# Two directions of a linear recurrence on the two halves of the array, row buffers at the end of three gathers, and two stages' loads

## The chip, the cores and the metric

The kernel runs on one core of a Trainium2 chip. The time is device microseconds (us), the median of repeated runs. TensorE is PE in the profile (its weight loads PEld), VectorE DVE, ScalarE ACT, GpSimd POOL, SyncE SP. SP, ACT and POOL issue the DMAs. All data are float32.

## The reference, cut to what matters

Two transformer blocks work on 256 tokens of width 1024. The first has two layers (with a context of 256 tokens in the first), each with a token mix and a product-key expert layer: every token picks 128 of 16384 experts, the kernel gathers their rows of two tables (4 KB each, "down" and "up"), takes the dot product of the token with each down row, puts it through gelu and a gate, and adds up the weighted up rows. The second block has attention, a bidirectional linear recurrence, and an expert layer of the same kind with its own tables.

```
def step(state, inp):                      # forward, and once more in reverse
    r_t, w_t, k_t, v_t, kk_t, a_t = inp
    sa = einsum('bhvk,bhk->bhv', state, -kk_t)
    state = (state * w_t[:, :, None, :]
             + sa[..., :, None] * (kk_t * a_t)[..., None, :]
             + v_t[..., :, None] * k_t[..., None, :])
    y = einsum('bhvk,bhk->bhv', state, r_t)
    return state, y
...
a = einsum('tkd,td->tk', peer_down[ee], hh)     # ee: 128 expert numbers a token
act = gg * gelu(a)
out = einsum('tk,tkd->td', act, peer_up[ee])
```

## The kernel before

Each engine has a class (`Vector`, `Tensor`, `Scalar`, `Pool`, `Sync`) that walks through the same `main` (L444) and emits only its own instructions. A stage is a generator; `weave` runs a front stage and puts `rate` units of a back stage between two of its steps, the same way on every engine, so the order of the work is fixed by the code and by that rate. PSUM has eight banks of 512 columns; a stage takes banks in turn from a ring (`step` has banks 0 to 2, `prep` 3 to 5), and waits until a bank's last reader has drained it. Weight blocks of 2 MB go into slots; slots 0 and 1 have memory of their own, slot 2 lies on the four buffers `K.ds`.

**Gathers.** `gather` handles one expert of all 128 tokens of a tile at a time: POOL fetches a down row and an up row, 0.5 MB each, into one of four buffers each (`K.ds`, `K.us`); DVE takes the dot product of the down row (L741); every 16 experts ACT applies gelu and DVE the gates; ACT makes a diagonal matrix of an expert's weights; PE multiplies it with the up row into PSUM (in odd tiles only the first half of the columns, the other half is DVE's). The up rows run 18 experts (`LAG`) behind the down rows, so at the end of each gather come 18 up rows alone. There are three gathers: four tiles, two tiles, and two tiles in the second block. `fold` ends a tile. Behind the first gather comes `x_second`, whose `modulate` starts with three vectors that ACT fetches (`take_vectors`).

**The recurrence** works on chunks of 32 tokens, with four heads of 32 tokens as 128 rows. The forward direction's 64 channels lie on partitions 0 to 63 and the reverse direction's on 64 to 127. A batch (`bt`, four of them) is two chunks of each direction. `prep` (L1995) makes what a batch needs that doesn't depend on the state: five gram products (`gram`), which DVE masks (`masked`), an inverse by powers of the masked matrix (`prod`), with evictions by ACT (`power`) and sums into `Q` by DVE. `steps` (L2074) runs through the chunks: a product with the state (`TA`, 64 rows) and `tl` times the values (128 rows), an eviction `UE` by DVE, the outputs into `b3`, and the state's update into `b2` (64 columns of the array), which DVE adds to the state and scales by the decay. `place` adds a chunk's outputs to two banks kept for that. `steps` of a batch is woven with `prep` of the next. The weave in front of it runs `recur` and the first `prep` with attention as its back.

**Behind it** come `close` (a group norm on DVE, and transposes), `project` with the weights `w_out_2` in two blocks, `modulate`, and the queries of the last gather.

## Time and profile before

| | |
|---|---|
| median of 3 runs | 4604.28 us (4602.84 to 4610.88) |
| the profiled execution | 4609.44 us |
| its span in the trace | 4607.6 us |
| PE busy | 3479.5 us (76%) |
| DVE busy | 2590.0 us (56%) |
| POOL busy | 1998.9 us (43%) |
| ACT busy | 831.7 us (18%) |
| mean DMA rate | 288 GB/s |

The trace counts a float32 matmul as two records and two weight loads. A row of the timeline gives the start, the length, the engine, the line of the kernel, the operation with its operands, how many it merges (x), and in brackets the idle time before it and what ended that. The first gather ends near 2150 us, the second near 3172, the recurrence runs from about 3453 to 3763, and the last gather ends near 4603.

### The profile page before, as it was taken

The page shows a single profiled execution, that of the slowest core. Times are in us where ns is not written, and L with a number is a line of the kernel's source. Part 1 is how long each engine was busy: PE and PEld are TensorE (multiplying, and loading weights), DVE is VectorE, ACT ScalarE, POOL GpSimd, SP SyncE. Part 2 cuts the span into 40 slices and gives each one's busy share as a digit, 9 for nine tenths or more (in the row PEclk, how much of TensorE's full clock was granted, in tenths as well). Part 3 has the DMA queues.
Part 4 walks back from the last instruction along what each step waited for, and adds up shares of the span by engine and source line. Part 5 has one row for each costly group of instructions (what it writes and reads, how often), then busy time and mean ns, then how long its engine had stood idle before and what let it go on. Part 6 is the DMA issues. An engine that isn't in the chain of part 4 may idle for free.

```text
span 4607.6 us, 34532 instructions
## 1 busy us (share of the span) xinstructions
PE 3479.5 (76%) x10470; PEld 1735.8 (38%) x10470; DVE 2590.0 (56%) x5497; ACT 831.7 (18%) x1973; POOL 1998.9 (43%) x2112
## 2 busy tenths in 40 slices
PE   6895868987786778876858766777679865877777
PEld 3483424553342235522434222212366643422111
DVE  1414695565877336674356755674443335667776
ACT  1311113111211122211211111111221101111111
POOL 0101666554666435574126764572000001676775
PEclk9997999988789889966979997757678987999656
DMA  5434999999999989998769998996000014999998
GB/s 188 170 148 167 360 342 358 360 377 341 382 338 374 373 327 344 407 400 315 245 222 353 401 386 314 403 407 234 12 1 1 1 52 164 348 402 361 405 408 341
DMA packets 385359, 1328.12 MB, mean 288 GB/s; under 512 B 38956, under 2 KB 44332, under 8 KB 381592
## 3 DMA queue, kind: packets, MB, share of 16 engines
q0 software_dynamic: 306432, 1115.88, 63.7%
q1 hardware_dynamic: 72592, 187.29, 11.0%
q10 hardware_dynamic: 6152, 22.74, 1.4%
q8 instruction: 87, 1.43, 0.1%
q14 instruction: 96, 0.79, 0.0%
HBM read 1324.59 MB, written 1.17 MB: 288 GB/s over the span
## 4 chain that ended last, share of the span: by engine, by line
PE 22%; DMA 14%; DVE 6%; POOL 5%; issue 4%; ACT 2%; DVEq 0%; ACTq 0%; POOLq 0%; SPq 0%
PE ps L1456 21%; DMA arena<-in_peer_up,arena 6%; POOL arena L2704 5%; DMA arena<-in_peer_v,arena 4%; DVE arena L728 3%; DVE arena L741 2%; ACT arena L2148 2%; DMA arena<-in_peer_u,arena 1%; DMA arena<-in_peer_down,arena 1%; PE ps L1462 1%; DMA arena<-in_ada_w 1%; DMA arena<-mod_scratch 0%; ACT L2148 0%; DVE arena L749 0%; DMA arena<-in_w_out 0%
## 5 line engine op out<-in xcount | busy, mean ns | idle before, releaser
L1456 PE MATMUL ps<-arena 128*128 128x512 f32 (+11 forms) x9732 | 3368.5, 522 | 902.9 <-DMA arena<-in_peer_up,arena 348.7
L1456 PEld LDWEIGHTS ps<-arena 128*128 128x128 f32 (+5 forms) x9732 | 1639.2, 197 | 2567.2 <-issue 1407.0
L741 DVE SCALAR_TENSOR_TENSOR arena<-arena,ps 128x1024 f32<-128x1024 f32 x1024 | 1240.9, 1216 | 512.1 <-DMA arena<-in_peer_down,arena 343.0
L2704 POOL DMA_INDIRECT arena<-in_peer_down,arena x768 | 740.7, 964 | 809.5 <-DVE arena L741 324.6
L2704 POOL DMA_INDIRECT arena<-in_peer_up,arena x768 | 731.5, 952 | 551.3 <-PE ps L1456 385.1
L2148 ACT ACTIVATE arena<-arena 128x128 f32<-128x128 f32 (+5 forms) x1250 | 448.2, 384 | 2009.7 <-PE ps L1456 953.8
L2704 POOL DMA_INDIRECT arena<-in_peer_u,arena x256 | 243.3, 950 | 817.5 <-DVE arena L745 724.2
L741 DVE SCALAR_TENSOR_TENSOR ps<-arena,ps 128x512 f32<-128x512 f32 x508 | 382.9, 754 | 147.5 <-DMA arena<-in_peer_up,arena 109.0
L2148 ACT ACTIVATE arena<-ps 128x512 f32<-128x512 f32 (+3 forms) x381 | 196.3, 515 | 1251.9 <-PE ps L1456 891.0
L728 DVE TENSOR_TENSOR arena<-ps,arena 128x512 f32<-128x512 f32 (+3 forms) x192 | 131.2, 683 | 472.7 <-PE ps L1456 430.7
L1462 PE MATMUL ps<-arena 128*128 128x128 f32 (+2 forms) x738 | 137.4, 326 | 219.2 <-DVE arena L728 152.2
L2704 POOL DMA_INDIRECT arena<-in_peer_v,arena x256 | 241.5, 944 | 128.0 <-PE ps L1456 87.7
L728 DVE TENSOR_TENSOR arena<-arena 128x512 f32<-128x512 f32 (+9 forms) x412 | 253.4, 615 | 45.1 <-ACT arena L2148 26.6
L728 DVE TENSOR_TENSOR arena<-arena,ps 128x256 f32<-128x256 f32 (+2 forms) x142 | 78.4, 552 | 309.8 <-PE ps L1456 286.6
L1462 PEld LDWEIGHTS ps<-arena 128*128 128x128 f32 (+2 forms) x738 | 101.4, 162 | 297.7 <-issue 187.5
L2148 ACT ACTIVATE arena<-ps,arena 128x256 f32<-128x256 f32 (+2 forms) x140 | 71.0, 507 | 416.7 <-PE ps L1456 380.7
L745 DVE COPY arena<-ps 128x512 f32<-128x512 f32 (+5 forms) x69 | 39.6, 574 | 173.3 <-PE ps L1456 142.5
L2148 ACT ACT_TABLE_LOAD x88 | 112.9, 1283 | 83.7 <-DVE arena L736 42.3
L2667 POOL DMA_DIRECT2D arena<-in_w_mod x16 | 12.5, 784 | 182.7 <-PE ps L1456 120.8
L1063 DVE MAX8 arena<-ps 128x8 f32<-128x128 f32 x128 | 28.7, 286 | 111.1 <-PE ps L1456 109.5
L741 DVE DVE_READ_ACCUMULATOR arena<-arena,ps 128x1 f32 x1024 | 83.9, 82 | 0.0
L741 DVE SCALAR_TENSOR_TENSOR arena<-arena 128x1024 f32<-128x1024 f32 (+6 forms) x67 | 46.8, 699 | 50.5 <-DMA arena<-mod_scratch 47.2
(35 smaller groups left out, 539.6 us busy)
## 6 DMA issues: line engine op xcount, KB each, us to landing
arena<-in_w_mod SPq DMA_DIRECT2D x16, 2048.0 KB, 18.2
arena<-in_gate_blocks SPq DMA_DIRECT2D x16, 2048.0 KB, 10.3
arena<-in_w_in SPq DMA_DIRECT2D x14, 2048.0 KB, 15.8
arena<-in_w_pq SPq DMA_DIRECT2D x12, 2048.0 KB, 10.1
arena<-in_ada_w POOLq DMA_DIRECT2D x24, 1024.0 KB, 5.7
arena<-in_w_mod POOLq DMA_DIRECT2D x16, 1024.0 KB, 6.0
arena<-in_w_out SPq DMA_DIRECT2D x8, 2048.0 KB, 13.2
arena<-in_gate_blocks SPq DMA_DIRECT2D x8, 1792.0 KB, 9.9
```

The lines of the kernel that those rows point to most:

```text
L728: self.e.tensor_tensor(o, a, b, op).then_inc(*(inc or self.inc(self.S.vec)))
L741: self.e.scalar_tensor_tensor(o, a, s, b, op0, op1, accum_out=accum).then_inc(*(inc or self.inc(self.S.vec)))
L745: self.e.tensor_copy(o, a).then_inc(*(inc or self.inc(self.S.vec)))
L1063: e.max(v[j][:, 0:8], src[j]).then_inc(*self.inc(S.vec))
L1456: return self.e.matmul(o, l, r, start=start, stop=stop)
L1462: ins = self.e.transpose(o, x, self.K.ident)
L2148: self.e.activation(o, i, f, bias=bias, scale=scale, accum_out=accum).then_inc(*(inc or self.inc(self.S.act)))
L2667: self.e.dma_start(K.wbuf[2][:, 2048 * half:2048 * half + 2048].rearrange("p (k n) -> p k n", n=512), rows[:, 4 * half:4 * half + 4, :]).t ...
L2704: self.e.indirect_dma_start(out=o, out_offset=None, in_=table, in_offset=bass.IndirectOffsetOnAxis(ap=idx.bitcast(U32), axis=0)).then_inc( ...
```

## The change

**The recurrence.** `grams` is a stage of its own in front of `prep`: five units, each with one gram product of both directions, the matmuls of the two directions in turn (one reads partitions 0 to 63, the other 64 to 127) and into two banks. The masked results of the reverse direction have memory of their own (`K.GRAM`). `prep` keeps eight units a direction. `steps` takes both directions of a chunk together: four units a batch instead of eight, the matmuls of the two directions in turn, one bank `b2` for both state updates, and one addition and one scaling on 128 partitions for both, with the decay copied into one tile first. The weave's rate goes from 2.25 to 5.25. `recur` orders its sums over time so that the directions take turns.

PE, one whole batch in the weave, as it was; here and below `free` is a bank drained, `128x256` a product of a step, `128x128` one of `prep` or a gram, `64x256` a state update and L1462 a transpose:

```order
L1456 MATMUL ps<-arena 128x128 x16
L1456 MATMUL ps<-arena 128x256 x4
L1456 MATMUL ps<-arena 128x128 x24
L1456 MATMUL ps<-arena 128x256 x6
L1456 MATMUL ps<-arena 64x256 x4
L1456 MATMUL ps<-arena 128x128 x4
```

and the batch's first half now, with what each waits for:

```order
L1492 MATMUL ps<-arena 128x256 [waits free1,state,free0,free4]
L1492 MATMUL ps<-arena 128x256 x7
L1492 MATMUL ps<-arena 128x512
L1492 MATMUL ps<-arena 128x512 [waits free2]
L1492 MATMUL ps<-arena 128x128 [waits free3]
L1492 MATMUL ps<-arena 128x128 x7
L1492 MATMUL ps<-arena 128x128 [waits free5]
L1492 MATMUL ps<-arena 128x128 x7
L1492 MATMUL ps<-arena 128x128 [waits free4,free3]
L1492 MATMUL ps<-arena 128x128 x7
L1492 MATMUL ps<-arena 128x256 [waits free1,free0]
L1492 MATMUL ps<-arena 64x256 x8
```

The products of a step stand in groups of eight and twelve, and the grams as five groups of eight in a row, each group behind the draining of banks 3 to 5.

PE, the last batch, where nothing is woven in, as it was:

```order
L1456 MATMUL ps<-arena 128x256 [waits state]
L1456 MATMUL ps<-arena 128x256 x3
L1456 MATMUL ps<-arena 128x512 [waits free0]
L1456 MATMUL ps<-arena 128x256 [waits state,free2]
L1456 MATMUL ps<-arena 128x256 [waits free1]
L1456 MATMUL ps<-arena 128x256 x5
L1456 MATMUL ps<-arena 64x256 x4
```

and now:

```order
L1492 MATMUL ps<-arena 128x256 [waits state,free1,free0]
L1492 MATMUL ps<-arena 128x256 x7
L1492 MATMUL ps<-arena 128x512
L1492 MATMUL ps<-arena 128x512 [waits free2]
L1492 MATMUL ps<-arena 128x256 [waits free1,free0]
L1492 MATMUL ps<-arena 128x256 x11
L1492 MATMUL ps<-arena 64x256 x8
```

A chunk waits once for the state instead of once per direction, and the twelve output products wait for both `UE` evictions (banks 0 and 1) at their start.

**The gathers.** The last 18 up rows go in turn into `K.us` and into the down buffers, which have no more down rows to take (`up_place`); POOL's waits follow that (`freed`), and a load into slot 2 waits until the up rows are used. Of the 19 fetches in a row with which a gather ends on POOL, four in the middle now wait for a dot product (`down`) and the others, as before, for an up row's use.

**Two stages' loads.** In the last tile of the first gather ACT also issues the three vectors of `x_second`'s `modulate`. SP issues the two blocks of `w_out_2` at the fence in front of `close`, not behind it, into slots 0 and 1.

```diff
+    def down_place(self, s):
+
+        x = self.base + LAG // 2 * self.gathers + s
+        return self.K.ds[x % ND], (self.S.down_in[x % ND], 16 * (x // ND + 1))
+
+    def up_place(self, u, total):
+
+        i = u - (total - LAG)
+        if i < 0 or i % 2 == 0:
+            x = self.base - LAG // 2 * self.gathers + (u if i < 0 else total - LAG + i // 2)
+            return self.K.us[x % NU], (self.S.up_in[x % NU], 16 * (x // NU + 1))
+        return self.down_place(total + i // 2)
 
     def folded(self, n):
...
-            self.weave(self.steps(bt % 2, bt), preps(bt + 1) if bt < 3 else iter(()), 2.25, rings=("step", "prep"))
+            self.weave(self.steps(bt % 2, bt), preps(bt + 1) if bt < 3 else iter(()), 5.25, rings=("step", "prep"))
         self.fence()
-        self.ring = self.rings["most"]
+        self.ring, self.slot = self.rings["most"], self.slots["two"]
         self.run(self.close())
         self.fence()
...
+        def masked(masks):
+            b = self.bank()
             self.wait_ge(*self.full(b))
...
+        for d in range(2):
+            masked(((d, K.GRAM[d]["L"]), (4 + d, K.GRAM[d]["LO"])))
+        yield
+        for d in range(2):
+            masked(((1 - d, K.GRAM[d]["Mt"]),))
+        yield
+        for d in range(2):
+            masked(((6 + d, K.GRAM[d]["LK"]),))
+        yield
+        for name in ("rb", "rk"):
+            for d in range(2):
+                masked(((3 - d, K.PD[bf][d][name]),))
+            yield
+
+    def prep(self, bf, d, chunks):
...
-                yield
+            decay = K.small[:, 8 * ci:8 * ci + 8]
             for d in range(2):
                 pr, c = slice(64 * d, 64 * d + 64), chunks_of(bt, d)[ci]
-                b2, b3 = self.bank(), self.bank()
-                self.wait_ge(*self.full(b2))
-                self.tt(K.ST[pr, :], K.ST[pr, :], b2.ap[pr, :], AD, inc=self.drain(b2))
-                pc = K.PI[pr, c, :, 31 if d == 0 else 0]
-                self.tt(heads(K.ST[pr, :]), heads(K.ST[pr, :]), pc.unsqueeze(2).to_broadcast([64, 8, 64]), M, inc=self.inc(S.state))
-                self.wait_ge(*self.full(b3))
-                self.tt(K.YE[d], groups(b3.ap), K.hb4, M, inc=self.drain(b3))
-                yield
+                self.copy(decay[pr, :], K.PI[pr, c, :, 31 if d == 0 else 0])
+            yield
+            b2, b3 = self.bank(), [self.bank() for _ in range(2)]
+            for d in range(2):
+                self.wait_ge(*self.full(b3[d]))
+                self.tt(K.YE[d], groups(b3[d].ap), K.hb4, M, inc=self.drain(b3[d]))
+            self.wait_ge(*self.full(b2))
+            self.tt(K.ST, K.ST, b2.ap, AD, inc=self.drain(b2))
+            self.tt(heads(K.ST), heads(K.ST), eight(decay), M, inc=self.inc(S.state))
+            yield
 
     def close(self):
         K, S = self.K, self.S
@@ -1838,14 +1874,16 @@
                 n, k = divmod(u, NEXT)
...
-                    for d in range(2):
-                        for i in range(4):
-                            h = 4 * hf + i
+                    for i in range(4):
+                        h = 4 * hf + i
+                        for d in range(2):
...
+        places = [(ci, g) for ci in range(2) for g in range(2)]
+        self.grammed = []
+        for l, r in ((K.AL, K.BE), (K.BE, K.AL), (K.AL, K.KA), (K.BE, K.RO), (K.KA, K.RO)):
+            banks = [self.bank() for _ in range(2)]
+            for b in banks:
+                self.wait_ge(*self.vacant(b))
+            for n, (ci, g) in enumerate(places):
+                for d in range(2):
+                    c = chunks_of(bt, d)[ci]
+                    i = self.mm(banks[d].ap[:, 128 * n:128 * n + 128], part(l, d, c, g), part(r, d, c, g), True, True)
+                    if n == 3:
+                        i.then_inc(*self.fill(banks[d]))
+            self.grammed.append(banks)
+            yield
...
+            made = [self.bank() for _ in range(2)]
+            for b in made:
                 self.wait_ge(*self.vacant(b))
+            self.states += 1
+            self.wait_ge(S.state, self.states)
+            for g in range(2):
+                n, cs = 2 * ci + g, slice(256 * g, 256 * g + 256)
+                for d in range(2):
+                    self.mm(made[d].ap[:, cs], K.TA[bf][pr[d], n, :], K.ST[pr[d], cs], True, False)
+                for d in range(2):
+                    i = self.mm(made[d].ap[:, cs], q[d]["tl"][:, n, :], q[d]["ve"][:, n, :], False, True)
+                    if g == 1:
+                        i.then_inc(*self.fill(made[d]))
+            self.place()
+            yield
+            b2, b3 = self.bank(), [self.bank() for _ in range(2)]
+            for b in b3:
+                self.wait_ge(*self.vacant(b))
+            for g in range(2):
+                n, cs = 2 * ci + g, slice(256 * g, 256 * g + 256)
+                for d in range(2):
+                    self.mm(b3[d].ap[:, cs], part(K.RO, d, chunks_of(bt, d)[ci], g), K.ST[pr[d], cs], True, False)
+                for d in range(2):
+                    self.mm(b3[d].ap[:, cs], q[d]["rk"][:, n, :], q[d]["ve"][:, n, :], False, False)
+                for d in range(2):
                     if g == 0:
                         self.wait_ge(*self.drained(made[d]))
+                    i = self.mm(b3[d].ap[:, cs], q[d]["rb"][:, n, :], ug[d][g], False, True)
+                    if g == 1:
+                        i.then_inc(*self.fill(b3[d]))
+            self.wait_ge(*self.vacant(b2))
+            for g in range(2):
+                n, cs = 2 * ci + g, slice(256 * g, 256 * g + 256)
+                for d in range(2):
+                    self.mm(b2.ap[pr[d], cs], q[d]["kr"][:, n, :], q[d]["ve"][:, n, :], True, False)
+                for d in range(2):
+                    i = self.mm(b2.ap[pr[d], cs], q[d]["br"][:, n, :], ug[d][g], False, True)
+            i.then_inc(*self.fill(b2))
+            self.placing = [(b3[d], chunks_of(bt, d)[ci], d) for d in range(2)]
...
+                if len(tiles) == 4 and u // NEXT == 3:
+                    self.take_vectors(1, K.A["norm1_g"][1], 0, 1)
+                    self.ahead = 1, 0
...
-                if c >= NU:
-                    self.wait_ge(S.up_tensor, c - NU + 1)
-                if self.halves(u - NU + 1):
-                    self.wait_ge(S.up_vector, self.halves(u - NU + 1))
-                self.fetch(K.us[c % NU], up, K.EI[:, tiles[n], k:k + 1], S.up_in[c % NU])
+                i = u - (total - LAG)
+                if i < 0:
+                    self.freed(max(0, u - NU + 1), total)
+                elif i >= 8:
+                    self.freed(u - 7, total)
+                elif i % 2 == 0:
+                    self.freed(total - LAG + i // 2 - NU + 1, total)
+                else:
+                    self.wait_ge(S.down, base + total + i // 2 - ND + 1)
+                o, there = self.up_place(u, total)
+                self.fetch(o, up, K.EI[:, tiles[n], k:k + 1], there[0])
...
+    def freed(self, n, total):
+
+        if self.base + n:
+            self.wait_ge(self.S.up_tensor, self.base + n)
+        if self.halves(n):
+            self.wait_ge(self.S.up_vector, self.halves(n))
...
+            self.wait_ge(self.S.up_tensor, self.base)
+            self.wait_ge(self.S.up_vector, self.shared)
...
-        if l == 2:
-            self.settled()
         for c in range(2):
-            self.block(self.K.A["w_out"][l] if l < 2 else self.K.A["w_out_2"][0], 512 * c, 512)
+            if l < 2:
+                self.block(self.K.A["w_out"][l], 512 * c, 512)
             yield from self.units_of(2)
+
+    def close(self):
+        self.settled()
+        for c in range(2):
+            self.block(self.K.A["w_out_2"][0], 512 * c, 512)
+        yield from self.units_of(2)
 
     def load_queries(self, l, blk):
```

## Rows read from the trace of the kernel before

**Rows 1.** Page: GB/s in 40 slices, and the chain by engine and line.

```profile
GB/s 188 170 148 167 360 342 358 360 377 341 382 338 374 373 327 344 407 400 315 245 222 353 401 386 314 403 407 234 12 1 1 1 52 164 348 402 361 405 408 341
...
PE 22%; DMA 14%; DVE 6%; POOL 5%; issue 4%; ACT 2%; DVEq 0%; ACTq 0%; POOLq 0%; SPq 0%
```

**Rows 2.** Busy time, granted clock, DMA share, GB/s of one weave.

```profile
3553.00:3643.00 90.00, 79.74 (x432) 57.35 (x432) 29.39 (x43) 13.04 (x24) 0.00 (x0) 0.96 0.00 1
```

**Rows 3.** Timeline of PE, one batch: start, length, engine, operation, [idle before].

```profile
3553.94 18.60 PE L1456 MATMUL ps<-arena 128*128 128x128 f32 x100 [1.50 <-DVE arena L728]
...
3584.47 1.16 PE L1456 MATMUL ps<-arena 128*128 128x128 f32 x8 [0.71 <-DVE arena L728]
...
3643.42 1.83 PE L1456 MATMUL ps<-arena 128*128 128x128 f32 x7 [1.50 <-DVE arena L728]
```

**Rows 4.** Weight loads (PEld) of the timeline; DVE's masks, grouped over the recurrence.

```profile
3513.78 0.29 PEld L1456 LDWEIGHTS ps<-arena 64*128 64x128 f32 x2 [0.33 <-issue]
...
3515.03 6.20 PEld L1456 LDWEIGHTS ps<-arena 64*128 64x128 f32 x50 [0.33 <-issue]
...
L728 DVE TENSOR_TENSOR arena<-ps,arena 128x512 f32<-128x512 f32 x79 | 54.6, 692 | 129.8 <-PE ps L1456 112.2 <-ACT arena L2148 15.3
```

**Rows 5.** Timeline of PE, last batch of the recurrence.

```profile
3737.71 17.51 PE L1456 MATMUL ps<-arena 64*128 64x256 f32 x60 [0.77 <-DVE arena L728]
...
3756.00 6.38 PE L1456 MATMUL ps<-arena 64*128 64x256 f32 x22 [0.77 <-DVE arena L728]
```

**Rows 6.** Stretches of 4 us: busy times and, third from last, granted clock.

```profile
3552.00:3556.00 4.00, 2.50 (x15) 2.34 (x15) 2.35 (x4) 0.36 (x1) 0.00 (x0) 0.80 0.00 0
...
3560.00:3564.00 4.00, 4.00 (x33) 3.76 (x32) 1.38 (x2) 1.19 (x2) 0.00 (x0) 1.00 0.00 0
```

**Rows 7.** Weight loads near the start: 32 columns wide, then full width.

```profile
43.26 0.20 PEld L1456 LDWEIGHTS ps<-arena 128*32 128x32 f32 x4 [0.66 <-issue]
...
64.02 0.34 PEld L1456 LDWEIGHTS ps<-arena 128*128 128x128 f32 x1 [0.52 <-issue]
...
66.70 0.19 PEld L1456 LDWEIGHTS ps<-arena 128*128 128x128 f32 x1 [0.24 <-issue]
```

**Rows 8.** Timeline of the second gather's tail; POOL's two rows last.

```profile
3133.07 0.37 SPq L2718 DMA_DIRECT2D arena<-in_w_in  x1
...
3135.26 0.40 ACT L2148 ACTIVATE arena<-arena 128x128 f32<-128x128 f32 x1 [1.67 <-DVE arena L728]
...
3136.97 0.76 DVE L741 SCALAR_TENSOR_TENSOR ps<-arena,ps 128x512 f32<-128x512 f32 x1 [0.54 <-DMA arena<-in_peer_up,arena]
...
3170.43 0.69 DVE L728 TENSOR_TENSOR arena<-ps,arena 128x512 f32<-128x512 f32 x1 [0.55 <-PE ps L1456]
...
3139.89 0.94 POOL L2704 DMA_INDIRECT arena<-in_peer_up,arena  x1 [0.30 <-issue]
3147.11 0.94 POOL L2704 DMA_INDIRECT arena<-in_peer_up,arena  x1 [6.28 <-DVE ps L741]
```

**Rows 9.** The same two moments of the first gather, and of the last.

```profile
2116.26 0.40 ACT L2148 ACTIVATE arena<-arena 128x128 f32<-128x128 f32 x1 [1.67 <-DVE arena L728]
...
2148.33 0.69 DVE L728 TENSOR_TENSOR arena<-ps,arena 128x512 f32<-128x512 f32 x1 [0.55 <-PE ps L1456]
...
4566.89 0.40 ACT L2148 ACTIVATE arena<-arena 128x128 f32<-128x128 f32 x1 [1.66 <-DVE arena L728]
...
4601.65 0.69 DVE L728 TENSOR_TENSOR arena<-ps,arena 128x512 f32<-128x512 f32 x1 [0.55 <-PE ps L1456]
```

**Rows 10.** Timeline of project in block two: its load, its first product.

```profile
3784.00 1.00 SPq L2718 DMA_DIRECT2D arena<-in_w_out  x2
...
3798.15 30.42 PE L1456 MATMUL ps<-arena 128*128 128x512 f32 x64 [15.08 <-DMA arena<-in_w_out]
```

**Rows 11.** Timeline behind the first gather: first modulate, first product.

```profile
2163.07 1.23 DVE L741 SCALAR_TENSOR_TENSOR arena<-arena 128x1024 f32<-128x1024 f32 x1 [11.87 <-DMA arena<-mod_scratch]
...
2176.18 5.81 PE L1456 MATMUL ps<-arena 128*128 128x160 f32 x40 [0.97 <-issue]
```

160 lines of the change are left out of this document (63 added, 97 removed).

## The prediction

> **What bounds the kernel now.** I read the page first. The chain that ended last is 22% PE, 14% DMA, 6% DVE [rows 1], so no engine sets the time everywhere. The change touches four stages, each read alone.
>
> *Recurrence.* The granted clock and busy times of one weave come first: in 90 us PE is busy 79.74 us at 0.96 of full clock, DVE 29.39, DMA idle [rows 2]. PE is the bound. One batch lasts 3643.42 - 3553.94 = 89.5 us [rows 3], with short PE waits of 0.7 to 1.5 us for DVE inside it, 10.3 us in all.
>
> *Gather tails.* After the last 16 gates are weighted (the ACT row at 3135.26), 16 rows remain. DVE could take one per 0.76 + 0.54 = 1.3 us, yet the fold starts only at 3170.43, 35.2 us later: POOL stops for 6.28 us in front of its fetch at 3147.11, because all four row buffers are taken [rows 8]. The last gather shows 34.8 us, the first 32.1 [rows 9].
>
> *Project of block two.* PE idles 15.08 us for w_out, issued at 3784.00, first product at 3798.15 [rows 10]. *First modulate after gather one.* DVE idles 11.87 us for vectors [rows 11].
>
> **A. The steps inside the weave (three batches).** A chunk (both directions) has 8 + 12 + 8 = 28 matmuls with 256 columns and 2 with 512. The trace shows each as two records, so 56 + 4. In the last batch, without preparation, a chunk takes 3756.00 - 3737.71 = 18.3 us, of which 17.5 is PE and 0.77 a wait [rows 5]. A 512-column record paces 0.19 + 0.24 = 0.43 us at full clock [rows 7], so 256 columns cost 0.215; 56 x 0.215 + 4 x 0.43 = 13.8. The other 3.7 us fall on 18 changes between matmuls with 64 rows, 128 rows and 64 columns: 0.2 each, seen as 0.33 us without a weight load where two weight loads for 128 rows end and the 64-row ones start [rows 4]. Side by side there are 9 changes: -1.9. If two halves of the array run at once, 16 records on row halves (state products) take the time of 8: -1.7; 16 on column halves (state updates) too: -1.7. So a chunk's PE time falls from 17.5 to 12.2, -5.3, or -10.6 a batch.
>
> Does the array run two halves at once? For columns the trace says yes: four 32-column records start per 0.20 + 0.66 = 0.86 us, where one full-width record needs 0.34 + 0.52 = 0.86 at the same half clock [rows 7]. For row halves no row shows it. Bounds: nothing gained, or half. I take half, as the nearest row (columns) has it. The Trainium skill ("TensorE: Matmul & The Clock Gate", Part 3 on packing) gives 3.07x for four row tiles and calls row and column tiles alike within some ns; by that the upper bound holds, and the column row above agrees.
>
> *Grams.* A batch has 10 gram products of 8 records. The 50 weight loads in 6.20 us [rows 4] make 0.124 a record, 1.0 a product, 9.9 us a batch, which lay between the power products and covered their evictions. Now five units of two products come in a row, each 1.0 us if paired. But DVE masks 12 results of 0.69 us (0.72 with the step between) [rows 4]: 8.7 us, behind two evictions of the step (1.4). The ring has three banks and a unit takes two: a unit waits for one mask of the unit before, so the cycle is 0.7 + 0.1 + 1.0 + 0.2 = 2.0, and with the first unit's four masks the burst ends 10.4 us after it began. So pairing the grams earns nothing: +0.5. Unpaired the same walk gives 14.8. The skill's page "TensorEngine Tiling (Array Packing)", PSUM Bottleneck, says that tiling speeds TensorE but not the evacuation of PSUM, which may then be the bound; by that page the halves' 5 us saved here are worth nothing, as in the walk, and no row of before can confirm it, since DVE is busy 29 of 90 us.
>
> *Clock.* Where PE waits, the granted clock falls: 0.80 in the 4 us from 3552, with PE busy 2.5 of them, and 1.00 again from 3560 [rows 6]. A burst that leaves PE idle half of 10 us invites more of it. Bounds: nothing, or the burst at 1.2 GHz (+4.4) and the 7 us behind it doubled (+7). I take +4.
>
> The power products lose the cover of the grams: two waits for evictions per direction, about 0.9 each (0.69 and two handovers of 0.1), less the one that a step now covers; the waits for Q (0.71) [rows 3] stay, and those of 1.5 shrink, as DVE has two state operations fewer per chunk. My count is 9 us against 10.3 before; I take 0. Sum a batch: -10.6 + 0.5 + 4 = -6, three batches **-18** (bounds -33 and +15).
>
> **B. Last batch alone.** PE 12.2 a chunk; the wait for the state grows: after the updates one add and one multiply on 128 partitions, 0.2 + 1.4 + 0.1 = 1.75, where the other direction's matmuls had covered one pair and left 0.77. The wait for the two evictions (b3 reuses their banks) is covered by the two 512-column placings. Chunk 14.0 for 18.3: two chunks **-8** (bounds -9, -2).
>
> **C. Before the recurrence.** Four sums over time alternate column halves, 16 records each, saving about 1 us each at 0.124; the first grams lose as much cover as above. I take **-2** (bounds -8, +4).
>
> **D. w_out in close.** Its load is now issued at the fence in front of close, near 3762.4 [rows 5], 21 us ahead of its use; it took 14 to 15 [rows 10]. The slots are now 0 and 1, free once the recurrence ends. The queries' first block, which had a free slot, must wait for the first half of project; it has then half of project and the modulate to land. **-14** (bounds -15, -10: this block late).
>
> **E. Tails.** A row is 0.5 MB, and the best slices move 408 GB/s [rows 1]: 1.3 us, which is DVE's pace too. With eight buffers, eight of the 16 rows lie ready when the weights come, and the ninth fetch has eight rows, over 10 us, to land. 16 x 1.3 = 20.6 plus 1 for the first products at half clock: 21.6 instead of 35.2 and 34.8: -13 each. The second gather loses one load of its tail: w_in, issued at 3133.07 [rows 8] into the memory of the down buffers, now waits for the end of the gather. It is used two blocks into the next stage. The first gather gets three vectors (1.5 MB, 4 us) into its tail: 32.1 - 21.6 - 4 = -6. Sum -32, of which I take **-31** (bounds -38, -15: POOL needs 0.94 + 0.30 us per fetch, and one late row stalls all).
>
> **F. Vectors ahead.** The 11.87 us wait [rows 11] goes; the squares, roots and an activation table load come last then, about 2 us. The next product needs w_in, still issued after the fence, but 1.5 MB less stands in front of it. Its 2176.18 moves by 9: **-9** (bounds -12, -4). ACT only issues these loads earlier, and its row buffers are free since the modulate in the third tile.
>
> Sum: -18 - 8 - 2 - 14 - 31 - 9 = -82. The profiled execution had 4609.4 us (span 4607.6), 0.1% over the median of 4604.3; 4609.4 - 82 = 4527, and for the median **4522**.
>
> **Rivals.**
> 1. *Row halves don't run at once.* For it: no row shows them. Chunks lose 1.7 eight times (+14), the gram burst lasts 14.8 (+4.4 three times): 4522 + 27 = 4549. Chance 0.18.
> 2. *The tails stay bound by landing.* For it: before, a fetch issued at 3139.89 into a fairly idle queue was not ready for over 4 us. Against: that is less than eight rows' work. Half of E: 4538. Chance 0.10.
> 3. *The moved loads buy nothing* (the stage waits for the next load behind): D and F lost, 4545. Chance 0.06.
> 4. *Slower: the clock.* The five gram units in a row starve PE in each batch, and the grant stays at 1.2 GHz through the recurrence. PE work of some 240 us at full clock would double, less some 50 us of waits that it fills: +190, against -82 elsewhere and here: 4712. It decides from the point where over a third of the recurrence runs at 1.2 GHz. Against: after the dip at 3552 the grant was 1.00 again 8 us later. Chance 0.04.
>
> The forecast holds 0.62. Range: with most bounds at their good end 4495; rivals 1 to 3 and a poor A reach 4560. Under 0.2% (9 us) a measurement of this kernel tells nothing from no change. Faster 0.93, same 0.03, slower 0.04.
>
> **What would show it.** Per batch about 83 us instead of 89.5; a chunk of the last batch 14 us; row-half records starting in pairs; DVE without gaps in the gram burst. About 22 us from the last weighting to each fold; no idle above 2 us on PE in front of project; 2163's wait gone. I am wrong if a batch takes over 88 us, if the tails keep over 28 us, or if PE waits at project for the load.

## The result, and the profile after

| | before | after |
|---|---|---|
| median | 4603.56 us (4600.6 to 4610.88, 4 runs) | 4491.59 us (4486.99 to 4500.99, 4 runs) |
| span of the profiled execution | 4607.6 us | 4493.3 us |
| PE busy | 3479.5 us | 3396.0 us |
| DVE busy | 2590.0 us | 2579.7 us |

The ratio is 0.9757, 95% interval 0.9736 to 0.9778. The prediction had 4522 us and a range from 4495 to 4560: right in sign and in most parts, too small by 30 us, and the measured time lies just below the range.

The span can be cut at moments that both traces have (the weighting and the fold of each gather, the first product of the steps, the load of w_out_2, the first product of project). The pieces add up to the 114.3 us between the two spans:

| piece | before | after | change | predicted |
|---|---|---|---|---|
| up to the first tail | 2116.3 | 2122.7 | +6.5 | 0 |
| three tails (E) | 32.1, 35.2, 34.8 | 27.4, 23.5, 24.6 | -26.6 | -31 |
| fold to the first product with w_in (F) | 27.9 | 18.4 | -9.5 | -9 |
| second fold to the first state (C) | 282.1 | 270.9 | -11.2 | -2 |
| three woven batches (A) | 272.5 | 224.3 | -48.2 | -18 |
| last batch (B) | 37.8 | 27.4 | -10.4 | -8 |
| close to project's first product (D) | 34.6 | 20.2 | -14.5 | -14 |
| the rest | | | -0.4 | 0 |

The first piece holds nothing that the change touches; in eight of the runs below its end lies anywhere from 2113.3 to 2124.4 us, so its 6.5 us are drift. So A alone is 30 of the 32 us by which the sum was off, C is 9 more, and E and the drift of the first piece take 11 back.

Two lists in the section on the change are shorter than their captions say. The one called a whole batch holds 14 products of a step with 256 columns, where a batch has 56; the one of the batch's first half holds three of the five groups of grams that its text counts.

Then the recurrence as a whole, from the first product of the steps to the end of the last batch. Columns: length, busy us of PE, PEld, DVE, ACT, POOL, the granted clock, DMA share, GB/s. Before:

```profile
3453.20:3763.50 310.30, 279.06 (x1414) 193.75 (x1414) 97.87 (x142) 39.31 (x73) 0.00 (x0) 0.95 0.00 1
```

After, that stretch, and one batch of it, which answers to [rows 2]:

```profile
3422.60:3674.30 251.70, 217.74 (x1416) 160.79 (x1416) 89.71 (x143) 39.35 (x73) 0.00 (x0) 0.95 0.00 1
3501.20:3576.00 74.80, 64.20 (x434) 48.66 (x432) 26.92 (x43) 13.05 (x24) 0.00 (x0) 0.95 0.00 1
```

PE's busy time fell by 61.3 us, its idle time (length less busy) only rose from 31.2 to 34.0, and the mean clock stayed at 0.95 (to two decimals; below it is taken apart). The timeline of PE after, where [rows 3, 5] were read: start, length, engine, line, operation, merged records, and idle before with its releaser.

```profile
3504.34 1.16 PE L1492 MATMUL ps<-arena 64*128 64x128 f32 x16 [1.50 <-DVE arena L748]
3506.75 1.16 PE L1492 MATMUL ps<-arena 64*128 64x128 f32 x16 [1.25 <-DVE arena L748]
3508.75 1.98 PE L1492 MATMUL ps<-arena 64*128 64x128 f32 x16 [0.84 <-DVE arena L748]
3511.53 11.92 PE L1492 MATMUL ps<-arena 64*128 64x128 f32 x72 [0.81 <-DVE arena L748]
...
3538.16 1.16 PE L1492 MATMUL ps<-arena 128*128 128x128 f32 x8 [0.34 <-DVE arena L748]
```

```profile
3646.84 12.18 PE L1492 MATMUL ps<-arena 64*128 64x256 f32 x60 [0.69 <-ACT arena L2195]
3660.63 14.09 PE L1492 MATMUL ps<-arena 64*128 64x256 f32 x64 [1.61 <-DVE arena L748]
```

```profile
3504.34 0.97 PEld L1492 LDWEIGHTS ps<-arena 64*128 64x128 f32 x16 [1.69 <-DVE arena L748]
```

16 records on row halves take 1.16 us (their weight loads, in the last row, 0.97) where 8 with 128 rows took as long before [rows 3] and 16 loads on one row half would take 16 x 0.124 = 1.98 [rows 4]: the row halves do run at once. The gaps between the gram units are waits for DVE's masks: 1.50 + 1.25 + 0.84 + 0.81 = 4.4 us a batch. The chunk of the last batch is 3660.63 - 3646.84 = 13.8 us (14.0 predicted), with the common state update's wait of 1.61 at its end (1.75 predicted). In stretches of 4 us, the clock of the same batch, to be held against [rows 6]:

```profile
3504.50:3508.50 4.00, 2.17 (x32) 1.81 (x32) 3.25 (x5) 0.00 (x0) 0.00 (x0) 1.00 0.00 0
3508.50:3512.50 4.00, 2.94 (x24) 2.71 (x26) 2.18 (x4) 0.00 (x0) 0.00 (x0) 0.55 0.00 0
3512.50:3516.50 4.00, 4.00 (x23) 3.05 (x20) 1.38 (x2) 0.00 (x0) 0.00 (x0) 0.60 0.02 4
3516.50:3520.50 4.00, 4.00 (x25) 2.54 (x25) 1.20 (x2) 0.00 (x0) 0.00 (x0) 1.00 0.00 0
```

PE is busy for 2.17 and 2.94 of 4 us in the burst, then the grant is at the lower level (1.2 GHz) for most of 8 us, and 1.00 again behind it.

The tails: the last weighting (ACT) and the fold (DVE) of gathers 2 and 3, as in [rows 8, 9], and three rows of DVE in the last one.

```profile
3127.49 0.40 ACT L2195 ACTIVATE arena<-arena 128x128 f32<-128x128 f32 x1 [1.66 <-DVE arena L748]
```

```profile
3151.00 0.69 DVE L748 TENSOR_TENSOR arena<-ps,arena 128x512 f32<-128x512 f32 x1 [0.55 <-PE ps L1492]
```

```profile
4466.75 0.75 DVE L761 SCALAR_TENSOR_TENSOR ps<-arena,ps 128x512 f32<-128x512 f32 x1 [1.56 <-DMA arena<-in_peer_v,arena]
4468.46 0.76 DVE L761 SCALAR_TENSOR_TENSOR ps<-arena,ps 128x512 f32<-128x512 f32 x1 [0.95 <-DMA arena<-in_peer_v,arena]
4470.54 0.75 DVE L761 SCALAR_TENSOR_TENSOR ps<-arena,ps 128x512 f32<-128x512 f32 x1 [1.32 <-DMA arena<-in_peer_v,arena]
...
4487.31 0.69 DVE L748 TENSOR_TENSOR arena<-ps,arena 128x512 f32<-128x512 f32 x1 [0.55 <-PE ps L1492]
```

Behind the last of these rows DVE keeps the pace of 1.3 us a row to the end, and POOL's pause of 6.28 us is gone. That pause hung on DVE, which itself waited for a row to land while the 2 MB of w_in, issued at 3133.07, were on their way; before:

```profile
3144.68 0.76 DVE L741 SCALAR_TENSOR_TENSOR ps<-arena,ps 128x512 f32<-128x512 f32 x1 [6.95 <-DMA arena<-in_peer_up,arena]
```

That load is now issued at 3150.97, behind the tail. So the second tail's gain holds the buffers and this load together, the third tail's (34.8 to 24.6) the buffers alone. The three rows of the last tail wait 1.56, 0.95 and 1.32 us for landings, against 0.53 elsewhere: 2.2 us over the pace, most of what 24.6 us has over the 21.6 of the prediction. The DMA engines were busy all the time then (a share of 0.98 and 1.00, 356 and 374 GB/s in the two stretches between 4464 and 4472).

D and F, as in [rows 10, 11]:

```profile
3674.32 0.99 SPq L2784 DMA_DIRECT2D arena<-in_w_out  x2
3711.21 0.37 SPq L2784 DMA_DIRECT2D arena<-in_peer_w_query  x1
```

```profile
3694.37 6.06 PE L1492 MATMUL ps<-arena 128*128 128x512 f32 x7 [0.97 <-issue]
```

```profile
2153.24 1.23 DVE L761 SCALAR_TENSOR_TENSOR arena<-arena 128x1024 f32<-128x1024 f32 x1 [0.27 <-ACT arena L2195]
```

PE starts project 0.97 us behind the transposes, with w_out_2 issued 20 us ahead. The modulate waits 0.27 us instead of 11.87. The queries' first block, now issued at 3711.21, holds nothing up.

### The profile page after: what moved, and what is told of

It reads as the page before. It is cut to its first block, busy times and chain, and to the rows that moved or that the text cites. A ratio compares the mean times of both kernels' runs of the same rounds, so it can differ in the third digit from the quotient of the medians.

```text
span 4493.3 us, 34522 instructions
## 1 busy us (share of the span) xinstructions
PE 3396.0 (76%) x10470; PEld 1688.0 (38%) x10470; DVE 2579.7 (57%) x5497; ACT 831.9 (19%) x1973; POOL 2003.4 (45%) x2112
## 3 DMA queue, kind: packets, MB, share of 16 engines
q8 instruction: 87, 1.43, 0.1%
## 4 chain that ended last, share of the span: by engine, by line
PE 21%; DMA 14%; DVE 6%; POOL 5%; issue 4%; ACT 2%; DVEq 0%; ACTq 0%; POOLq 0%
PE ps L1492 20%; DMA arena<-in_peer_up,arena 6%; POOL arena L2768 5%; DMA arena<-in_peer_v,arena 5%; DVE arena L748 3%; DVE arena L761 2%; ACT arena L2195 2%; DMA arena<-in_peer_down,arena 2%; DMA arena<-in_peer_u,arena 1%; PE ps L1498 1%; DMA arena<-in_ada_w 1%; DVE arena L769 0%; ACT L2195 0%; DMA arena<-mod_scratch 0%; DVE arena L1104 0%
## 5 line engine op out<-in xcount | busy, mean ns | idle before, releaser
L1492 PE MATMUL ps<-arena 128*128 128x512 f32 (+11 forms) x9732 | 3283.9, 520 | 878.8 <-DMA arena<-in_peer_up,arena 334.8
L1492 PEld LDWEIGHTS ps<-arena 128*128 128x128 f32 (+5 forms) x9732 | 1590.8, 197 | 2507.9 <-issue 1337.8
L748 DVE TENSOR_TENSOR arena<-arena 128x512 f32<-128x512 f32 (+8 forms) x404 | 247.6, 613 | 50.6 <-ACT arena L2195 25.5
L748 DVE TENSOR_TENSOR arena<-arena,ps 128x256 f32<-128x256 f32 (+1 forms) x134 | 73.0, 545 | 273.7 <-PE ps L1492 252.0
L761 DVE SCALAR_TENSOR_TENSOR arena<-arena 128x1024 f32<-128x1024 f32 (+6 forms) x67 | 46.8, 699 | 37.8 <-DMA arena<-mod_scratch 34.2
## 6 DMA issues: line engine op xcount, KB each, us to landing
arena<-in_w_mod SPq DMA_DIRECT2D x16, 2048.0 KB, 19.2
arena<-in_gate_blocks SPq DMA_DIRECT2D x16, 2048.0 KB, 10.3
```

Source lines behind the costliest of these rows:

```text
L748: self.e.tensor_tensor(o, a, b, op).then_inc(*(inc or self.inc(self.S.vec)))
L761: self.e.scalar_tensor_tensor(o, a, s, b, op0, op1, accum_out=accum).then_inc(*(inc or self.inc(self.S.vec)))
L1492: return self.e.matmul(o, l, r, start=start, stop=stop)
```

## The experiments

The first question was why A came out at -16.1 us a batch and not at -6. Each kernel stands beside runs of the kernel before on its own chip. The chips differ (the kernel before took 4604 to 4740 us), so totals are given as ratios, and the recurrence is compared by its own stretch, from the first product of the steps to the issue of w_out_2 (L below; 251.7 us after, 251.0 when run again, 310.3 before to the same point in the program).

L can be split in three. Cut it into 100 equal stretches and take in each PE's busy time times (1 - granted clock): their sum is what the lower level (1.2 GHz, a grant of 0.50) cost. The rest of PE's busy time is its work at full clock, and the rest of L is its idle time.

| us | L | work | clock | idle |
|---|---|---|---|---|
| before | 310.3 | 263.5 | 15.5 | 31.2 |
| after | 251.7 | 207.7 | 10.1 | 33.9 |
| grams set apart | 257.7 | 214.9 | 16.8 | 26.0 |
| single masks twice | 264.0 | 207.1 | 16.4 | 40.5 |
| steps set apart | 283.0 | 230.5 | 19.2 | 33.2 |
| fewer changes of form | 249.2 | 203.7 | 12.4 | 33.1 |
| grams spread | 240.7 | 208.9 | 3.3 | 28.6 |
| steps alone | 252.3 | 224.3 | 1.6 | 26.5 |
| grams alone | 287.4 | 247.1 | 10.3 | 30.0 |
| spread, set apart | 244.1 | 217.1 | 4.7 | 22.3 |
| spread and order | 233.1 | 203.7 | 1.7 | 27.8 |
| spread wide, and order | 230.8 | 204.1 | 4.6 | 22.1 |

Five further runs have the recurrence of the changed kernel unaltered (the changed kernel again and the four that put back tails, loads or sums). Over these and the changed kernel L is 251.0 to 254.4, the work 207.4 to 208.1, idle 33.7 to 34.0, and the clock's cost 9.0 to 13.0. So work and idle are good to half a microsecond, while a difference in L or in the clock's cost of under 4 us may be chance.

**Do two halves at once pay in the grams?** In `grams` the loops change places:

```diff
-            for n, (ci, g) in enumerate(places):
-                for d in range(2):
+            for d in range(2):
+                for n, (ci, g) in enumerate(places):
```

> The changed kernel, with the five gram units as they are but in each unit the eight records-pairs of one direction first and then those of the other, so that two row halves are never next to each other. Theory (the row halves run at once, and the masks on DVE pace the burst of grams): a unit's matmuls take 1.98 us instead of 0.97. By the walk in the prediction the burst grows from 10.4 to 14.8 us, +4.4 in each of the three woven batches; the first preparation, which shares its time with attention, +4. Total +17 (4509 us for the 4492 of the changed kernel), and DVE, not PE, has the longer gaps in the burst. Rival (PE's waits for the masks hide a slower unit, since DVE needs 1.4 us a unit): below +6. Rival 2 (the halves don't run at once, the short start-to-start times in the records say nothing on the work): 0.

```profile
3503.17:3760.87 257.70, 231.66 (x1416) 174.49 (x1416) 89.74 (x143) 39.34 (x73) 0.00 (x0) 0.93 0.00 1
```

Ratio 0.9776 (0.9759 to 0.9794) against 0.9757. L grew by 6.0 us, 2.0 a batch, and the stretch in front of the first state by 6.2 us: +12, between the theory's 17 and the first rival's 6. PE's busy time grew by 13.9, but only 7.2 of it (2.4 a batch) is work, 6.7 is the lower clock; idle time fell by 7.9. So the halves run at once, and DVE's masks take back all of the pairing's work: what L lost is about what the clock cost more. The theory also had the unit too long. Set apart it took 1.68 us instead of 1.16, and its 16 weight loads 1.52 instead of 0.97, not 1.98:

```profile
3590.16 1.68 PE L1492 MATMUL ps<-arena 64*128 64x128 f32 x16 [0.70 <-DVE arena L748]
```

So this edit doesn't undo the whole gain of the halves; why a unit with one change of direction is faster than 16 times 0.124 was not tested.

**Do the masks pace the burst?** The single masks are applied twice:

```diff
+            masks = masks * 2 if len(masks) == 1 else masks
             for n, (mi, dst) in enumerate(masks):
```

> The changed kernel, with each single mask of the grams applied twice (eight more DVE operations of 0.72 us in each batch: two in the second unit and two in each of the three behind it). Theory (the masks set the pace of the burst): about 6 of the 8 x 0.72 = 5.8 us come out, a little less where DVE waits for PE now (0.5 to 1.4 us a unit): +2.5 to +4 a batch, three batches +8 to +12 from the first product of the steps to w_out_2's issue. Rival (PE's own matmuls and handovers set it, DVE has room): below +3.

```profile
3506.18:3770.17 263.99, 223.47 (x1416) 165.39 (x1416) 106.30 (x167) 39.34 (x73) 0.00 (x0) 0.92 0.00 1
```

Ratio 0.9808 (0.9784 to 0.9833). L +12.3 us, 4.1 a batch, for 5.8 of DVE's work: a little above the theory's band. But only 6.6 us of it, 2.2 a batch, are waits; 6.3 are the lower clock (0.92 for 0.95). The four waits for masks between the units of a burst grew from 4.4 to 6.6 us, and PE's work stayed. So the masks do pace the burst, as the walk in the prediction had it, for a part of their length, and the clock doubles the price.

**Do the halves pay in the steps?** All matmuls of one direction, then those of the other (core of the edit, first unit; the second likewise):

```diff
-            for g in range(2):
-                n, cs = 2 * ci + g, slice(256 * g, 256 * g + 256)
...
+            for d in range(2):
+                for g in range(2):
+                    n, cs = 2 * ci + g, slice(256 * g, 256 * g + 256)
+                    pair = [(K.TA[bf][pr[d], n, :], K.ST[pr[d], cs]), (q[d]["tl"][:, n, :], q[d]["ve"][:, n, :])]
+                    for x, (l, r) in enumerate(pair if g else pair[::-1]):
+                        i = self.mm(made[d].ap[:, cs], l, r, x == 0, x == 1)
```

> The changed kernel, with the steps' matmuls by direction: all of the forward direction, then all of the reverse one, in an order with 10 changes of form a chunk (9 in the changed kernel), so that two row halves, or two column halves, of different directions are never next to each other. Banks, units, evictions and the common state update stay. Theory (two halves at once save half of 32 records of 0.215 us): +3.4 us a chunk and +0.2 for the tenth change, eight chunks: +29, 4521 us; the last batch's chunk 17.4 us instead of 13.8. Rival (the gain of a chunk came from fewer changes of form and from the common state update, the halves give nothing): +2, 4494 us, chunk 14.0.

The last chunk's PE row, to be held against the row at 3660.63 after (64 records in 14.09 us), and L:

```profile
3757.37 16.89 PE L1492 MATMUL ps<-arena 128*128 128x256 f32 x64 [1.60 <-DVE arena L748]
```

```profile
3490.90:3773.85 282.95, 249.72 (x1416) 182.43 (x1416) 89.75 (x143) 39.35 (x73) 0.00 (x0) 0.92 0.00 1
```

Ratio 0.9844 (0.9826 to 0.9861). L +31.2, where the theory had 29 and the rival 2. The chunk went from 13.8 to 16.6 us, 2.8 instead of 3.6; the clock (0.92 for 0.95, +9.1 us) made up the rest. PE's work grew by 22.8 us, 2.85 a chunk. Less the tenth change of form (0.2), row and column halves together are worth 2.6 us a chunk; the terms of the prediction had 3.4.

**What does a change between forms cost?** The accumulations are turned so that matmuls of one form meet:

```diff
+                for x, state in enumerate((True, False) if g else (False, True)):
...
+                for x, name in enumerate(("RO", "rk", "rb") if g else ("rk", "rb", "RO")):
```

> The changed kernel, with the order of each accumulation turned so that matmuls of one form meet: values, state, state, values in the first unit and rk, rb, RO, RO, rk, rb in the second, directions in turn as before. 6 changes of form a chunk instead of 9, the first two matmuls of a chunk need no state, but rb waits for the evictions two matmuls earlier. Theory (a change costs 0.2 us): -0.6 us a chunk for the changes, -0.4 where the state was waited for, +0.2 for rb: -0.8, eight chunks -6: 4486 us; the last batch's chunk 13.0 us. Rival (a change costs nothing that isn't hidden by the matmuls' own length): within 2 us of 4492, chunk 13.8.

```profile
3722.85 13.50 PE L1492 MATMUL ps<-arena 128*128 128x256 f32 x64 [0.79 <-DVE arena L748]
```

The last batch's chunk fell from 13.8 to 12.4 us, and the wait for the state from 1.61 to 0.79 (the first two matmuls need no state). In the half of a woven batch that no mask paces, from the transposes in front of the second chunk's first unit to the next batch, 42.53 us (3528.84 to 3571.37) became 41.74 (3593.75 to 3635.49) with the same waits: there the units stand between matmuls with 128 rows, and four changes fall out, not three, 0.2 us each. But L fell only from 251.7 to 249.2. In the half with the burst only one change falls out, since the grams next to the units have 64 rows themselves. That makes 5 a woven batch and 6 in the last, 21 x 0.2 = 4.2 us; PE's work fell by 4.0. The clock cost 2.3 us more, within its spread from run to run. Its level in one burst:

```profile
3569.00:3573.00 4.00, 2.12 (x22) 1.66 (x18) 2.60 (x4) 0.00 (x0) 0.00 (x0) 0.72 0.00 0
3573.00:3577.00 4.00, 2.99 (x24) 2.75 (x26) 2.10 (x4) 0.00 (x0) 0.00 (x0) 0.50 0.00 0
3577.00:3581.00 4.00, 4.00 (x19) 3.24 (x17) 1.38 (x2) 0.00 (x0) 0.00 (x0) 0.50 0.02 4
```

Ratio 0.9751 (0.9732 to 0.977).

**Does the burst cost the clock?** Two gram units stay in front, the other three go one by one behind the first units of the forward preparation:

```diff
-            yield from self.grams(bt % 2, bt)
+            grams = self.grams(bt % 2, bt)
+            for _ in range(2):
+                yield next(grams)
             for d in range(2):
-                yield from self.prep(bt % 2, d, chunks_of(bt, d))
+                for n, unit in enumerate(self.prep(bt % 2, d, chunks_of(bt, d))):
+                    yield unit
+                    if (d, n) in ((0, 0), (0, 1), (0, 2)):
+                        yield next(grams)
```

> The changed kernel, with the last three gram units (K times A, and the two for the outputs) no longer in a row behind the first two, but one behind each of the first three units of the first direction's preparation. Work and pairing stay. Theory (the burst costs 4.4 us of PE's waits for masks and about 3 us at the lower clock in each woven batch, and spread they cover the waits for ACT's evictions): -3 to -6 us a batch with the first one, -12 to -24 in total: 4468 to 4480 us, with no stretch of 4 us below 0.80 of full clock. Rival (a pair of grams takes two of the ring's three banks, so it waits for the power products' evictions itself, and the waits only change place): within 4 us of 4492.

```profile
3583.00:3587.00 4.00, 2.85 (x32) 2.53 (x30) 3.07 (x5) 0.63 (x2) 0.00 (x0) 1.00 0.00 0
3587.00:3591.00 4.00, 4.00 (x38) 3.40 (x39) 1.39 (x2) 1.75 (x3) 0.00 (x0) 1.00 0.01 4
```

```profile
3503.95:3744.70 240.75, 212.15 (x1416) 156.23 (x1416) 89.72 (x143) 39.35 (x73) 0.00 (x0) 0.99 0.00 1
```

Ratio 0.9739 (0.972 to 0.9757). L 240.7, 11.0 us less or 3.7 a batch, inside the theory's 3 to 6: 6.8 us less for the clock, 5.3 less idle, 1.2 more work. The preparation in front of the first state gained nothing (272.5 us), so the total stays just under the theory's 12. The grant is 1.00 where it was 0.55 and 0.60, and 0.99 over all.

**Steps alone, grams alone.** What each half of the recurrence's change does without the other: first the preparation as before with the steps side by side, then the grams in front with the steps as before.

```diff
-            yield from self.grams(bt % 2, bt)
...
-            self.weave(self.steps(bt % 2, bt), preps(bt + 1) if bt < 3 else iter(()), 5.25, rings=("step", "prep"))
+            self.weave(self.steps(bt % 2, bt), preps(bt + 1) if bt < 3 else iter(()), 4.5, rings=("step", "prep"))
...
+        b1, b2 = gram(K.AL, K.BE), gram(K.BE, K.AL)
```

> The changed kernel with the preparation of the kernel before (ten gram products between the power products, each direction by itself, 18 units a batch at a rate of 4.5); the steps are side by side. From the first product of the steps to w_out_2's issue 251 to 252 us in the changed kernel, 308 in the kernel before counted to the same point. Theory (the steps earn what the prediction had, 5.3 a chunk, and the grams' new place the rest): the weaves and the last batch 3 x 10.6 + 10.4 = 42 shorter than before, 17 longer than the changed kernel: 268. Rival (the steps earn nearly all, since they also take four units and two waits for the state out of a batch): 256 or less. In front of the first state: 8 to 10 us longer than the changed kernel (279 to 281), as the grams are not paired there.

```diff
+            self.weave(self.steps(bt % 2, bt), preps(bt + 1) if bt < 3 else iter(()), 2.625, rings=("step", "prep"))
...
-            made = [self.bank() for _ in range(2)]
+            made = []
+            for d in range(2):
+                q, pr = K.PD[bf][d], slice(64 * d, 64 * d + 64)
+                b = self.bank()
```

> The changed kernel with the steps of the kernel before (one direction after the other, eight units a batch, two state updates), and the grams of both directions paired in a row ahead of the preparation (rate 2.625). Theory: the grams' part is -5.5 a batch, the steps' part 10.6 a batch and 10.4 in the last is lost: 251.5 + 42 = 293 us to w_out_2's issue. Rival (the grams' place earns nothing by itself, as the prediction had it, +0.5 and +4 for the clock): 308 or more. In front of the first state: as the changed kernel, 271.

```profile
3509.90:3762.20 252.30, 225.81 (x1416) 168.97 (x1416) 89.68 (x143) 39.31 (x73) 0.00 (x0) 0.99 0.00 1
3588.07:3663.00 74.93, 66.78 (x434) 51.06 (x432) 26.94 (x43) 13.03 (x24) 0.00 (x0) 1.00 0.00 1
```

```profile
3516.20:3803.60 287.40, 257.38 (x1414) 173.77 (x1414) 97.97 (x143) 39.34 (x73) 0.00 (x0) 0.96 0.00 1
```

Ratios 0.9782 (0.9762 to 0.9801) and 0.9853 (0.9831 to 0.9874). Here my theory fell: the steps alone bring L to 252.3 us, as far as the whole change, and the rival was right on the amount. The grams alone give -22.9 (287.4, where the theory had 293 and the rival 308 or more). Together they give 58.6, not 81. PE's work adds up (39.2 and 16.4 us saved alone, 55.8 together). The clock and the waits do not: 13.9 and 5.2 us saved on the clock alone, 5.4 together; idle 4.7 and 1.2 us less alone, 2.7 more together. With the steps alone the grant is 0.99 over L and 1.00 in the batch shown, against 0.95 before and after. In front of the first state the run with the steps alone was 276.1 us, 5.2 more than after (the theory had 8 to 10).

**Spread, with the matmuls of a unit apart.** The loops of the first experiment on top of the spread:

> The changed kernel with the last three gram units spread as in the earlier experiment, and each unit's matmuls one direction after the other. With the burst the pairing was worth 2 us a woven batch (5.9 over three, instead of the 4.9 a batch that its matmuls save), because DVE's masks paced it. Theory (where the units are spread PE is the bound and the pairing earns its matmul time in three of five units): 3 to 4 us a batch over the spread kernel's 260.5, 270 to 272 us from the first product of the steps to project. Rival (masks and evictions still pace): 266 or less.

```profile
3424.80:3668.90 244.10, 221.81 (x1416) 165.98 (x1416) 89.69 (x143) 39.31 (x73) 0.00 (x0) 0.98 0.00 1
```

Ratio 0.9736 (0.9719 to 0.9753). L 244.1, 3.3 above the spread kernel (263.8 us from the steps to project); the rival was right. The pairing saves 8.2 us of work here and 1.4 on the clock, and 6.3 of that goes into waits: 1.1 us a batch are left, no more than L's spread from run to run. The spread saves its time through the waits and the clock, not through the matmuls.

**Sums over time in the old order.**

```diff
-                    for i in range(4):
-                        h = 4 * hf + i
-                        for d in range(2):
+                    for d in range(2):
+                        for i in range(4):
+                            h = 4 * hf + i
```

> The changed kernel with the four sums over time in the old order, one direction's four matmuls and then the other's. Theory (column halves side by side take half the time: 16 records in 1.1 us where one direction after the other takes 2.8 at the lower clock and 2.0 at full clock): 3.5 to 4 us more in the stretch between the second fold and the first state. Rival (the 11 us gained in front of the recurrence come from these sums, since they stand on the way of everything behind them): 8 or more. Rival (all of it is from the first preparation, the sums are covered by DVE): 1 or less.

Second fold to first state 272.3 us instead of 270.9, close to the last rival. Ratio 0.9753 (0.9735 to 0.9771). But the changed kernel and seven runs whose code is the same between these marks show 270.5 to 272.9, so the old order of the sums shows no effect. The preparation's grams do: 276.1 us with the grams of the kernel before and 277.1 with the units set apart, above all of these. Against the spread the first is 3 to 6 us. The rest of C's 11.2 us is open.

**The other parts put back.** Four buffers in the tails (`up_place` and POOL's waits as before):

> The changed kernel with four buffers for the up rows of the three tails. Theory (the fifth to the eighth buffer take 4.7 to 11.7 us out of each tail, 26.6 together, as the two traces have it): 27 us more than the changed kernel, ratio to before about 0.9815, the last tail 34 to 35 us from the last weighting to the fold. Rival (the first tail, which now also holds three vectors, hides part): the first tail at 36 or more, 30 us or more in sum. Rival (most of the difference was drift of the DMA rate between the two runs): below 15.

```profile
2123.85 0.40 ACT L2192 ACTIVATE arena<-arena 128x128 f32<-128x128 f32 x1 [1.67 <-DVE arena L745]
```

```profile
2162.83 0.69 DVE L745 TENSOR_TENSOR arena<-ps,arena 128x512 f32<-128x512 f32 x1 [1.79 <-PE ps L1489]
```

Tails of 39.0, 35.9 and 33.7 us against 27.4, 23.5 and 24.6: 33 us in the profiles, and the first rival was right about the first tail, which holds the vectors. This kernel also issues w_in inside the second tail again, at 3137.96, so only the third tail's 9.1 us are the buffers' alone. The ratio of 0.9803 (0.9784 to 0.9822) puts the total at 21 us against the changed kernel's 0.9757, and at 17 against the 0.9767 that it has on this chip; the profiled execution of this kernel was 12 us slower than its median. I take 17 to 33.

The loads where they were (`take_vectors` in the last tile left out, w_out_2 back in `project`):

> The changed kernel with the three vectors and w_out_2 fetched where the kernel before does it; buffers of the tails stay eight. Theory: the wait for vectors and what follows comes back (+9.5), w_out_2 too (+14.5), and the first tail loses the 1.5 MB of the vectors, 27.4 to about 24 us (-3.5): +20, ratio to before about 0.980. Rival (the first tail is not slowed by the vectors; it stays at 27 because its eight buffers fill late): +24.

```profile
2138.93 0.69 DVE L748 TENSOR_TENSOR arena<-ps,arena 128x512 f32<-128x512 f32 x1 [0.55 <-PE ps L1492]
...
2153.46 1.23 DVE L761 SCALAR_TENSOR_TENSOR arena<-arena 128x1024 f32<-128x1024 f32 x1 [11.66 <-DMA arena<-mod_scratch]
```

The wait of 11.66 us is back. The first tail is 2138.93 - 2114.92 = 24.0 us, so the vectors cost it 3.4, as the theory had it (4 in the prediction). The stretch from the steps' start to project grew by 13.2. Ratio 0.9797 (0.9782 to 0.9813), +14 to +18, by the same two ratios, for the +20 expected.

Only the recurrence changed:

> The changed kernel with the gathers' buffers, the three vectors and the load of w_out_2 as in the kernel before: only the recurrence and its sums are changed. Theory (the parts add up; in the two traces the recurrence, what lies in front of it from the second fold, and the last batch became 11.2 + 48.2 + 10.4 = 70 us shorter): 70 us less than the kernel before, a ratio of 0.985. Rival (what the recurrence gained is given back by another part that the change also touches, such as the load of w_out_2 which now would be needed earlier): less than 60 us, 0.987 or more.

Ratio 0.988 (0.9862 to 0.9897), 57 us less than before. The theory's 70 and its ratio of 0.985 lie outside the interval, and the rival's numbers (less than 60, 0.987 or more) fit. Its mechanism is not shown, though: the wait for w_out_2 is 15.20 us, as before. In its trace the stretch before the first state is 272.9 us (-9.1) and from the steps to project's first product 3731.36 - 3442.69 = 288.7 (344.9 before, -56.3), together -65. So the stretches add up within 5 us in the traces, while the medians show some 9 us less, and which other stretch differed stays open.

**A kernel that beats both.** The changed kernel again, then spread and order together, then with the fourth and fifth gram unit in the reverse direction's preparation:

> The changed kernel itself, as the measure for the three beside it on this chip. Ratio to the kernel before 0.974 to 0.978; from the first product of the steps to the first of project 271.8 us.

> The changed kernel with the edits of two earlier experiments together: the last three gram units spread between the first direction's units, and the steps' accumulations in the order with 6 changes of form a chunk. Theory (the order saved 0.6 us in each chunk that no mask paces and 1.4 in the last batch, but nothing where the longer half-clock stretch took it back; without that stretch it earns everywhere): the spread's 11 us from the first product of the steps to project, and 5 more: 256 us instead of 271.8, ratio to the changed kernel 0.9965. Rival (the waits for masks and evictions fill what the order saves): 260 us, as with the spread alone.

> As the run with spread and order, but the third gram unit stands behind the first unit of the forward direction's preparation and the fourth and fifth behind the first two of the reverse direction's, so that both directions have work between their power products. Theory (a gram unit covers an eviction wait of 0.7 to 0.8 us wherever it stands, and the reverse direction's waits are open in the changed kernel): 2 to 3 us more saved over three batches, 254 us. Rival (a unit of two banks in a ring of three waits for the evictions itself, so its place doesn't matter once DVE has room): 256 us, the same.

| on one chip | median | ratio to before | steps to project |
|---|---|---|---|
| changed kernel | 4496.29 us | 0.9767 (0.9749 to 0.9785) | 271.0 us |
| spread and order | 4469.21 us | 0.9712 (0.9693 to 0.9731) | 252.8 us |
| spread wide, and order | 4468.93 us | 0.9704 (0.9682 to 0.9725) | 250.5 us |

```profile
3417.40:3650.50 233.10, 205.31 (x1416) 156.45 (x1416) 89.71 (x143) 39.34 (x73) 0.00 (x0) 0.99 0.00 1
```

The order, which earned 2.6 us with the burst, earns 7.6 on top of the spread, more than both predicted stretches (256 and 260) allow: 5.2 of work instead of 4.0, 0.8 of idle time in both, and 1.6 on the clock where it had cost 2.3. The clock's part lies within its spread from run to run. The wide spread takes 2.3 us more in the stretch, as its theory had it (5.7 of idle time, less 2.9 for the clock), which the medians can't tell.

## Why the prediction was wrong in size

**The steps of A that failed** are the clock, "I take +4", and the waits: the burst's 5.4 us that stand in "So pairing the grams earns nothing: +0.5", and "My count is 9 us against 10.3 before; I take 0". PE's work was right. The predicted terms, sorted as L is split above, beside the two single edits in both orders:

| us, three batches and the last | predicted | measured | steps, then grams | grams, then steps |
|---|---|---|---|---|
| PE's work at full clock | -57 (8 x 5.3 and 3 x 4.9) | -55.8 | -39.2, -16.6 | -16.4, -39.4 |
| the clock | +12 | -5.4 | -13.9, +8.5 | -5.2, -0.2 |
| PE idle | +18 (3 x 5.4 and 2 x 1.0) | +2.7 | -4.7, +7.4 | -1.2, +3.9 |
| sum | -27 | -58.6 | -58.0, -0.6 | -22.9, -35.7 |

*Work.* The steps were to save 42.4 us and saved 39; the grams 14.7, and saved 16.5. Both come out the same in either order. The chunk of the last batch came out at 13.8 for 14.0, halves at once are worth 2.6 of the 3.4 us in it, changes of form 0.2 each.

*Clock.* The prediction had the mechanism (a burst in which PE starves pulls the grant down) and nearly its price: on top of the steps alone the burst costs 8.5 us, 2.8 a batch. But the kernel before paid 15.5 us already, which the 0.80 of [rows 6] and the 0.96 of [rows 2] showed; I added the new dip and left the old ones standing. With the side-by-side steps alone the old dips were gone (1.6 us); what in the old order of the steps made them was not tested. Of the 5.4 us that the whole change saved on the clock some may be chance, but the sign of the forecast was wrong. A forecast of the clock has to be a difference of two states of the kernel, and I had only one.

*Waits.* The walk of the burst was near: at full clock the units follow each other after 2.4 and 2.0 us (3504.34, 3506.75, 3508.75), and the burst holds 4.4 us of PE's waits where 5.4 were predicted. The sign "DVE without gaps in the gram burst" did not hold: it pauses 0.51 us between two units' masks at full clock and 1.30 and 1.43 at the lower level. Wrong was the rest of the batch. The batch after idles 10.6 us, so 6.2 stand outside the burst, where I had counted 9 and booked no change; before, the batch held 9.7. Part can be seen, a wait for `Q` of 0.79 at 3609.60 with the steps alone that is 0.34 after; which waits make up the rest was not separated.

*Banks.* The Trainium skill ("TensorEngine Tiling (Array Packing)", PSUM Bottleneck) says that tiling speeds TensorE and not the evacuation of PSUM. The runs agree: doubling the masks added 2.2 us of waits a batch, and of the 2.4 us of work a batch that pairing saves against the units set apart, the waits took all.

**B** (-10.4 for -8): two chunks gave 2 x (18.3 - 13.8) = 9.0; the other 1.4 us lie at the batch's ends and were not traced. **C** (-11.2 for -2) failed on "the first grams lose as much cover as above": they saved 3 to 6 us instead. The sums, 4 us in the forecast, show no effect. **D** and **F** (-14.5 for -14, -9.5 for -9) came out as worked out. **E** (-26.6 for -31) had the pace right (1.3 us a row) and missed 2 to 3 us in each tail in which the rows that should lie ready were still landing; "eight of the 16 rows lie ready" was too much while the DMA engines were busy all the time. (16 x 1.3 is 20.8, not 20.6; the 21.6 stands with it.) Rival 1 is refuted by the row-half records and by the steps apart, rival 2 and rival 3 by the tails and the two loads. The row that rival 2 leaned on was misread: between 3140 and 3144 the queue moved 376 GB/s, it was not idle. Rival 4's mechanism is real, but the lower level costs 10 us over L, not 190, and less than before.
